# Linear attention on one core: per-level decays by products on VectorE instead of exponentials of sums

## The reference, cut to what matters

```python
def gla_log_decay(lowrank, w_up, b):
    gk = (lowrank @ w_up + b).astype(jnp.float32)
    return (jax.nn.log_sigmoid(gk) / GATE_NORM).reshape(B, L, GLA_HEADS, GLA_DK)

def step(S, inp):                       # one chunk of tokens, one direction
    qc, kc, vc, ac = inp
    b = jnp.cumsum(ac, axis=2)
    bC = b[:, :, -1:, :]
    S_new = jnp.exp(bC[:, :, 0, :, None]) * S + jnp.einsum(
        'bhjd,bhjv->bhdv', kc * jnp.exp(bC - b), vc)
    diff = b[:, :, :, None, :] - b[:, :, None, :, :]
    decay = jnp.exp(jnp.where(tri[:, :, None], diff, -jnp.inf))
    scores = jnp.einsum('bhid,bhjd,bhijd->bhij', qc, kc, decay)
    o = jnp.einsum('bhij,bhjv->bhiv', scores, vc) + jnp.einsum(
        'bhid,bhdv->bhiv', qc * jnp.exp(b), S)
    return S_new, o
```

## Time and profile before

| what | us |
| --- | --- |
| runs shown | 3113.21, 3122.37, 3106.71 |
| their median | 3113.21 |
| the profiled execution's own time | 3106.99 |
| its span, first to last instruction | 3105.2 |
| stage P, 334.5 to 720.9 | 386.4 |
| stage S, 720.9 to 860.6 | 139.7 |
| stage F, 860.6 to 1137.2 | 276.6 |
| busy over the span: TensorE, VectorE, GpSimd, ScalarE | 2773.8, 1410.6, 947.5, 744.3 |

### The profile page before, as it was taken

The page is one execution under the profiler, slowest core; times in us unless marked ns, Lnnn a source line. Parts: engine busy times, 40 slices in busy tenths (PEclk is TensorE's granted clock), DMA queues, the critical chain, the costliest instruction groups (busy, mean ns, idle before and its releaser), DMA issues.

```text
span 3105.2 us, 36143 instructions
## 1 busy us (share of the span) xinstructions
PE 2773.8 (89%) x12500; PEld 2180.5 (70%) x12500; DVE 1410.6 (45%) x2057; ACT 744.3 (24%) x1109; POOL 947.5 (31%) x449
## 2 busy tenths in 40 slices
PE   2899999999968768999669998999879999999997
PEld 1688777778757655777358676667747777777775
DVE  7774122221157757651339434544143544444446
ACT  2311233331023225320231123544031110001102
POOL 1243333333213342443025230000223443334444
PEclk8899999999979888999879996988989999999999
DMA  7465444445454433222201011212201111111111
GB/s 264 161 226 190 165 170 169 169 156 194 171 186 139 166 131 140 81 88 96 80 27 41 27 33 55 62 53 61 88 27 41 48 42 48 47 47 47 41 47 68
DMA packets 124934, 317.77 MB, mean 102 GB/s; under 512 B 11584, under 2 KB 42880, under 8 KB 124224
## 3 DMA queue, kind: packets, MB, share of 16 engines
q1 hardware_dynamic: 72576, 197.31, 19.0%
q10 hardware_dynamic: 52288, 119.52, 10.7%
HBM read 243.77 MB, written 73.01 MB: 102 GB/s over the span
## 4 chain that ended last, share of the span: by engine, by line
PE 50%; issue 5%; DVE 5%; ACT 1%; DMA 1%; DVEq 0%; ACTq 0%
PE pb L432 39%; PE g L2199 3%; PE g L2165 2%; PE g L469 2%; PE g L2181 1%; PE pb L2167 1%; PE g L2056 1%; DMA x<-xp_d 1%; DVE zcs L1622 0%; PE g L2147 0%; DVE x L1872 0%; DVE hl L1813 0%; PE g L2096 0%; DVE xin L1331 0%; ACT ptr L1148 0%
## 5 line engine op out<-in xcount | busy, mean ns | idle before, releaser
L631 POOL TENSOR_TENSOR w_hi<-w_raw,one 128x1024 fp32r<-128x1024 f32 x177 | 349.8, 1976 | 1929.0 <-PE pb L432 1896.9
L432 PE MATMUL pb<-xh,w_hi 128*128 128x512 f32 (+1 forms) x1400 | 545.0, 389 | 69.1 <-DVE xl L1327 68.2
L432 PE MATMUL pb<-xh,w_lo 128*128 128x512 f32 (+1 forms) x1400 | 537.7, 384 | 0.0
L432 PE MATMUL pb<-xl,w_hi 128*128 128x512 f32 (+1 forms) x1400 | 537.7, 384 | 0.0
L634 POOL TENSOR_TENSOR w_lo<-w_raw,w_hi 128x1024 fp32r<-128x1024 f32 x177 | 477.0, 2695 | 13.9
L432 PEld LDWEIGHTS pb<-xh,w_hi 128*128 128x128 f32 x1400 | 265.3, 189 | 135.8 <-issue 81.0
L432 PE MATMUL pb<-mh,w_hi 128*128 128x512 f32 x832 | 334.1, 402 | 27.9 <-DVE ml L1327 23.0
L432 PE MATMUL pb<-mh,w_lo 128*128 128x512 f32 x832 | 332.5, 400 | 0.0
L432 PE MATMUL pb<-ml,w_hi 128*128 128x512 f32 x832 | 332.1, 399 | 0.0
L432 PEld LDWEIGHTS pb<-xl,w_hi 128*128 128x128 f32 x1400 | 265.5, 190 | 57.4
L432 PEld LDWEIGHTS pb<-xh,w_lo 128*128 128x128 f32 x1400 | 266.2, 190 | 55.1 <-issue 0.5
(11 more groups left out here) (270 smaller groups left out, 4279.0 us busy)
## 6 DMA issues: line engine op xcount, KB each, us to landing
w_raw<-in_wall SPq DMA_DIRECT2D x177, 512.0 KB, 3.5
mod_raw<-in_modw SPq DMA_DIRECT2D x72, 512.0 KB, 5.6
proj_d<-stage ACTq DMA_DIRECT2D x44, 512.0 KB, 2.7
at_bias<-in_bias SPq DMA_DIRECT2D x64, 256.0 KB, 2.6
proj_d<-stage ACTq DMA_DIRECT2D x13, 640.0 KB, 3.4
fla<-la_d SPq DMA_DIRECT2D x8, 1024.0 KB, 5.5
svt<-vt_d ACTq DMA_DIRECT2D x12, 512.0 KB, 4.4
vc<-proj_d ACTq DMA_DIRECT2D x10, 512.0 KB, 4.6
```

Source lines behind the costliest of these rows:

```text
L432: mm = pe.matmul(pb[bank][:, 0:n], w[:, b, wc:wc + P], x[:, k, tokens], start=(count == 0), stop=(count == total - 1))
L631: nc.gpsimd.tensor_tensor(w_hi[:, b, :], w_raw[:, b, :], one[:, 0:1].to_broadcast([P, 1024]), ALU.mult).then_inc(w_high, 1)
```

## The change

It replaces sums of log decays and their exponentials by products of the decays themselves.

Stage P now keeps the decay `av` (ScalarE takes the exponential of the log decay, 2 x 512 elements). VectorE runs a product along the tokens (`tensor_tensor_scan`, 516 elements, one for each direction), and multiplies the keys with it (`kd`). TensorE transposes eight blocks of `kd` in place of four of the keys; the matmuls with triangular matrices go. The gate's argument is made transposed, by eight small matmuls. Queries are rotated here and no longer in stage F, so `p_load` has thirteen transfers for a token chunk (eight for the context's), and it stands *behind* the first tile's copies. Queries are scaled as their projection is copied out.

Stage F no longer has `f_exponents`, the exponentials or the rotation. VectorE makes the factors of level l+1 from those of level l with the products over blocks (`span`): 33 instructions with those of `f_first` and `f_last`, 25 of them of 256 elements. ScalarE copies what a level leaves as it is (`f_kept`, two copies of 256 elements for a level, three at level 0). All picks come last, from four PSUM banks instead of two. SyncE issues 7 loads for a chunk in place of 10 (2.36 MB in place of 3.07 MB), and the loads of `tabq` and `lev` at the start of the stage go (2.1 of 2.6 MB). The loops over chunks are written out.

```diff
 act side, stage P
-                if more:
-                    act.wait_ge(p_kt, c + 1)
-                    p_load(i * 2 + (b + 1), 1 - b)
                 p_tile(i, 3 * b)
+                if after is not None:
+                    act.wait_ge(p_kt, c + 1)
+                    act.wait_ge(p_out[1 - b], i * 80 + (80 + 80 * b))
+                    p_load(i * 2 + (b + 1), 1 - b, after)
                 act.wait_ge(p_gk, c + 1)
...
-                act.wait_ge(p_la, c + 1)
-                act.activation(lah[:, b], la[:, :, :], ACT.Copy).then_inc(p_lah, 1)
+                act.wait_ge(p_la, c + 2)
+                for d in range(2):
+                    act.activation(av[:, b, d, :, d:d + CH],
+                                   soft[:, d, :].rearrange("p (h n) -> p h n", n=CH), ACT.Exp,
+                                   scale=1.0 / GATE_NORM).then_inc(p_av, 1)
...
 dve side, stage P
+                    nc.vector.tensor_tensor_scan(
+                        backward[0], backward[1], view(reset[:, :, :], 0, (1, H + HEADS)), 0.0,
+                        ALU.mult, ALU.add).then_inc(p_run, 1)
+                dve.wait_ge(p_kr, c + 1)
+                for d in range(2):
+                    dve.wait_ge(p_run, i * 4 + (2 * b + d + 1))
+                    v = nc.vector.tensor_tensor(kd[:, d], kc[:, b], run[:, d, :, 1 - d:1 - d + CH], ALU.mult)
+                v.then_inc(p_kd, 1)
...
 pe side, stage P
+                p_tile(i, 3 * b + 1)
+                pe.wait_ge(p_kd, c + 1)
                 pe.wait_ge(p_kt, c + 1)
...
+                        mm = pe.transpose(g[:, 2 + 3 * d, CH * h:CH * h + CH], kd[:, d, h, :], ident)
+                mm.then_inc(p_ktr, 1)
                 p_tile(i, 3 * b + 2)
...
 act side, stage F
+            def f_chunk(c):
+                b = c % 2
+                for l in range(4):
+                    f_kept(c, l)
+                if c:
+                    f_out(c - 1)
+                act.wait_ge(f_lev, 8 * c + 1)
+                act.wait_ge(f_omm, c + 1)
+                act.activation(pt[:, :, :].rearrange("p h n -> p (h n)"), g[:, 2, :], ACT.Copy, scale=2.0)\
+                   .then_inc(f_diag, 1)
+                for l in (4, 5):
+                    f_kept(c, l)
...
 dve side, stage F (f_grow: one level)
+                nc.vector.tensor_tensor(outer(lq[:, l + 1], m), outer(lq[:, l], m), factor(s + 1, 1 - s),
+                                        ALU.mult).then_inc(f_rec, 1)
+                nc.vector.tensor_tensor(outer(lk[:, l], m), outer(lkl, m), factor(1, s + 1),
+                                        ALU.mult).then_inc(f_rec, 1)
+                nc.vector.tensor_tensor(span[l + 1][:, :, :], view(t, 0, (s, 2), (2, s // 2)),
+                                        view(t, 1, (s, 2), (2, s // 2)), ALU.mult).then_inc(f_rec, 1)
+                dve.wait_ge(f_cpy, CPY * c + 2 * l + 1)
+                nc.vector.tensor_tensor(inner2(bq[:, :, :], m), inner2(lq[:, l], m), factor(0, s + 3),
+                                        ALU.mult).then_inc(f_rec, 1)
...
+            for c in range(NCX):
+                f_first(c)
+                for l in range(LEVELS - 1):
+                    f_grow(c, l)
+                f_last(c)
+                if c:
+                    f_update(c - 1)
                 for l in range(LEVELS):
+                    f_choose(c, l)
```

More of the change, by code:

```diff
@@ new lines, in rope, with p_chunk @@
+                nc.vector.tensor_tensor(swapped, swapped, sin, ALU.mult).then_inc(p_dve, 1)
+                dve.wait_ge(p_dve, seen)
+                nc.vector.tensor_tensor(x, x, swapped, ALU.add).then_inc(ready, 1)
+            def p_chunk(i, b, queries):
+                c = i * 2 + b
+                dve.wait_ge(p_in[b], i * 208 + (208 if queries else 128))
+                if queries:
+                    rope(c, kc[:, b], ks[:, b], i * 8 + (4 * b + 2), p_kr)
+                    rope(c, qc[:, b], qs[:, b], i * 8 + (4 * b + 4), p_qr)
+                else:
+                    rope(c, kc[:, b], ks[:, b], 4 * NCX + 2 * b + 2, p_kr)
@@ L1371, in p_chunk @@
-                dve.wait_ge(p_exp, c + 2)
-                dve.wait_ge(p_ktr, c + 1)
-                nc.vector.tensor_tensor(kt[:, b, 0, :], ef[:, 0, :], g[:, 2, :], ALU.mult)
-                nc.vector.tensor_tensor(kt[:, b, 1, :], ef[:, 1, :], g[:, 2, :], ALU.mult).then_inc(p_kt, 1)
-            with dve.Fori(0, NC // 2) as i:
+                dve.wait_ge(p_kt, c + 1)
+                for d in range(2):
+                    dve.wait_ge(p_av, i * 4 + (2 * b + d + 1))
+                    step_, last = (-1, H + HEADS - 1) if d == 0 else (1, 0)
+                    backward = [view(x, last, (step_, H + HEADS)) for x in (run[:, d], av[:, b, d])]
+                    nc.vector.tensor_tensor_scan(
+                        backward[0], backward[1], view(reset[:, :, :], 0, (1, H + HEADS)), 0.0,
+                        ALU.mult, ALU.add).then_inc(p_run, 1)
@@ new lines, in f_last @@
+            def f_last(c):
+                b, top = c % 2, span[LEVELS - 1][:, :, :]
+                dve.wait_ge(f_rec, rec(c, 5, 3))
+                dve.wait_ge(f_cpy, CPY * c + 12)
+                for d, first in ((0, 0), (1, 9)):
+                    half = slice(64 - 64 * d, 128 - 64 * d)
+                    nc.vector.tensor_tensor(qi[:, b, d, :, half], lq[:, LEVELS - 1, :, half],
+                                            view(top, first, (2, HEADS), (0, 64)), ALU.mult)\
+                      .then_inc(f_rec, 1)
@@ new lines, in f_chunk @@
+                pe.wait_ge(f_in[b], 112 * (c // 2 + 1))
+                scores(0, fk[:, b], fq[:, b])
+                for l in range(LEVELS):
+                    pe.wait_ge(f_rec, REC * c + 1 if l == 0 else rec(c, l - 1, 2))
+                    if l:
+                        pe.wait_ge(f_cpy, CPY * c + 2 * l)
+                    if l == 3:
+                        pe.wait_ge(f_diag, c + 1)
+                    if l > 3:
+                        pe.wait_ge(f_pred, 7 * c + l + 4)
+                    scores(l + 1, lk[:, l - 1] if l else fk[:, b], lq[:, l])
```

389 lines of the change are left out of this document (169 added, 220 removed).

## The result

The changed kernel takes 3177.43 us (median of 4 runs, 3169.83 to 3193.62), the kernel before 3117.79 (4 runs, 3106.71 to 3123.36): a ratio of 1.0203, 95% interval 1.0152 to 1.0254, or some 60 us more. A repeat of both, as the first experiment, gave 1.0197. The forecast was +42 us.

A forecast was written before the change was run, and what follows sets the result against it. TensorE was taken to bound stage P, and two chains, the attention's and that of SyncE with GpSimd, to end stage F together. Stage P +47 and stage F -5 gave +42 on 3113.21: 3155 us, range 3104 to 3181.

The forecast's parts named there:

- TensorE's own work in stage P: Stage P: transposes and gate matmuls replace the old extras on TensorE, 3.7 us a chunk, 1.0 less than before.
- The wait for `kd`: Stage P: TensorE idles 5.4 us (4.8 to 6.0) before transposing `kd` in chunks 1 to 6, 2.5 in 7 and 8.
- The clock: Stage P: TensorE restarts at a lower clock after each 5.4 us stall, costing 2.3 us (0 to 3.0).
- Stage F, the start: Start of stage F: fewer bytes to load, so the load of chunk 2 goes 16.6 us sooner.
- Tile 1: Stage F, the moving average's tile 1: about -1 us.
- Stage F, the cycles: Stage F, tiles 2 to 6: GpSimd shut out by VectorE's run, 180.1 us against 163.1, +17.0.
- Tile 7: Stage F, last tile of the average: no chunk beside it, so it loses the earlier blocking, -4.3 us.
- Everything behind stage F: All stages after stage F: the forecast had no term for them.
- Rival A: Stage F: GpSimd gets in between VectorE's products; stage F gains 41 us, total +6, 3119 us; chance 0.27.
- Rival B: Stage P: ScalarE's transfers don't hold the gate's chain; stage P gains 10 us, total 3098 to 3062 us; chance 0.10.
- Rival C: Stage F: VectorE's factors or ScalarE hand-overs take longer; stage F +20, total +67, 3180 us; chance 0.08.

The follow-up runs named there:

- the first experiment: The changed kernel once more, unchanged, against the kernel before: 3178.15 us, ratio 1.0197 (1.0152 to 1.0241).

## Why the prediction was wrong

The forecast was 3155, and the change came out at 3177, near the upper end of the range. Two steps failed: stage F was forecast at -5 us and took +10.6, and all that follows it was put at nothing and took some 12 us by the medians. A stage P that lost 10 us less than forecast hid part of it. Step by step:

- **TensorE's own work in stage P, -1.0 us a chunk: too small.** 37.1 against 38.8 in the run with early loads, -1.7.
- **The wait for `kd`, 5.4 us: right,** 5.45 to 5.47 in chunks 1 to 5, 5.2 in chunk 6, 2.7 and 2.8 in chunks 7 and 8 (2.5), none in the last. Inside it two errors met: a scan takes 1.18 us and not 0.95, and the transfers 6.9 and not 7.4. The Trainium skill (DVE: opcode table, instruction layouts, handler registers and perf-mode slots, section 6) has this scan at "half throughput", and the trace agrees: 516 elements in 1.18 us, where products of 512 pitch at 0.6.
- **The clock, 2.3 us a stall: too large,** 1.65. TensorE worked for some 3.3 us at the lower level, where the earlier trace rows had 6.0 and I took three quarters; chunk 8 kept its clock behind its wait of 2.8 us and lasts only 1.3 us more than before. With the term before, a full stall comes to 5.46 + 1.65 - 1.7 = 5.4 us, and the chunk of 44.3 us is 5.5 over 38.8. The sum of +47 for the stage became +37, by the right mechanism.
- **Stage F, the start, -16.6: it was -11.4.** The load of chunk 2 went out at 943.57, 43.2 us in. GpSimd was shut out in the second half of tile 0 as well, for 9.33 us, which I had not counted. It is so in the repeat too (9.40). In the runs with early loads and with pauses in the convolution it isn't, and there the load of chunk 2 goes out 37.3 and 38.2 us in, as forecast (38). Tile 1 took +3.2 in place of -1.
- **Stage F, the cycles, +17.0: they were +23.1,** 186.2 us for tiles 2 to 6 against 163.1. The mechanism was right to a few tenths (VectorE 1.4 us ahead where 1.7 was forecast, the pause 9.85 us into the run where 9.3 was), but tile 2 took 3.0 us more than its term and the others 0.4 to 1.1. Tile 7 gave back 4.7 (4.3). The terms now add up: -11.4 + 3.2 + 23.1 - 4.7 = +10.2 where -5 stood.
- **Everything behind stage F, 0: a term put at nothing without a reason but that its code is the same.** In the two profiles it was +36 and +20. Of this, 10 us is the split of the weight tile in the convolution: the mechanism that I had priced for stage F, at work in a stage that I hadn't looked at. The rest is the lower granted clock in the attention. The first profile, the longest of its runs, has more of it than most: by the medians, 60 us less the 37 and 11 of stages P and F leaves 12. Why the clock is lower there stays open.

**The rivals.** Rival A (GpSimd gets in) was wrong for the change and right for the kernel with pauses: stage F gained 33 us there where the rival had 41. The Trainium skill (SBUF — State Buffer, Who interferes with whom) says that the holder has the shared ports "for the whole instruction". Here GpSimd can be held for longer than one instruction: in stage F, with no pause in VectorE's stream, GpSimd waits through 23 instructions and more, 9.4 us, and in the convolution once for 27.7, and in stage F a gap of 0.1 us in the pitch lets it in. In the convolution it also got in without one, in 2.0 to 3.0 us. Rival B fell: thirteen transfers held the Abs for 6.9 us. It became true in effect, at -12.7 us in stage P, as soon as the transfers moved. Rival C had the sign of stage F's loss, at twice its size (+20 for +10.6), and not its cause, since VectorE's run was longer than priced by no more than 0.7 to 1.0 us.

## What to carry to other kernels

Where a change puts a new chain behind an engine's transfers, count the issue time that now stands in front of its first step: here 6.9 us of issues on ScalarE turned a gain of 13 us into a loss of 38. Where it makes VectorE's stream denser, look for GpSimd in every stage, those with unchanged code too, and give it a pause a few times in a run that nobody waits for; never one behind each instruction of a run that is waited for. And before taking a slower time as a verdict on the arithmetic, undo the order alone: with the order of two queues and a few pauses mended, this one came out 1.7% faster.

## What the runs showed of the hardware that I had not expected

- In the kernel before with late loads, TensorE waited 0.3 us ahead of four matmuls of 512 columns and sixteen of two, and was then granted 0.55 for 3.4 us; without the wait it had 1.00 there. It was so in seven chunks of ten; in an eighth, a wait of 0.28 us left it at 1.00.
- How long GpSimd's instruction is held does not depend on its size: 8.3 us for 40 columns and for 527 (8.58 and 9.37 us, less the 0.25 and 1.06 us of work).
- In one run of 60 products of VectorE with no pause (pitch 1.20 us) GpSimd's split got in five times within 2.0 to 3.0 us and was then held for 27.7.
- VectorE's products of 256 elements pitch at 0.34 us, but at 0.55 at the first level (1024.38 to 1027.18 in the changed kernel), where an operand is read from `fa`, and those of 512 in `f_first` at 0.75. The seven products in the earlier trace rows had shown no such difference.
- The same 1558 matmuls took 338, 352, 368 or 382 us at a granted clock of 0.82, 0.79, 0.75 or 0.71, by the profile, with the two longest in changed kernels alone. What decides between them stays open.
